# Order of the products in w_up: each 512-column product with the 256-column product of its tile behind it

## The reference

```python
h = rms_norm(x, norm_ffn_g[i])
u = causal_dwconv(h @ w_up[i], ffn_conv_w[i])      # w_up: 2048 x 11264, convolution of 3 taps
u_g, u_v = jnp.split(u, 2, axis=-1)
x = x + (jax.nn.silu(u_g) * u_v) @ w_down[i]       # w_down: 5632 x 2048
```

## Time and profile before

| | |
|---|---|
| time, median of 3 runs | 1561.92 us (1561.05 to 1563.58) |
| time of the profiled execution | 1562.31 us |
| its span, first to last instruction | 1560.6 us |
| TensorE products | 7667, busy 1552.0 us |
| w_up, first stretch | 736.0 to 1004.9 us |
| w_up, second stretch | 1131.4 to 1354.2 us |
| products of w_up | 1408 of 512 columns (L614), 1408 of 256 columns (L620) |

### The profile page before, as it was taken

One profiled execution on the slowest core, in us unless ns is written; L12 is line 12 of the kernel. 1 busy time (PEld: TensorE's weight loads), 2 busy tenths in 40 slices (PEclk: granted clock), 3 DMA queues, 4 the chain that ended last, 5 costly groups with the idle time before them and its releaser, 6 DMA issues.

```text
span 1560.6 us, 20864 instructions
## 1 busy us (share of the span) xinstructions
PE 1552.0 (99%) x7667; PEld 1311.8 (84%) x7667; DVE 1141.2 (73%) x1366; ACT 815.4 (52%) x970; POOL 80.4 (5%) x120
## 2 busy tenths in 40 slices
PE   9999999999999999999999999999999999999998
PEld 7878888888888888888888888888888888888887
DVE  5599867766676557678678778778767777787754
ACT  6355454544554445456555455555545555555543
POOL 5000110000000011000000101000000010000000
PEclk9999999999999999999999999999999999999999
DMA  7656655666655688665677767666677776575564
GB/s 256 209 169 193 195 175 175 189 183 194 196 179 173 200 233 256 205 204 195 200 219 226 215 217 242 206 221 222 218 213 214 207 224 215 193 231 192 189 199 150
DMA packets 167818, 319.66 MB, mean 205 GB/s; under 512 B 11287, under 2 KB 16131, under 8 KB 167744
## 3 DMA queue, kind: packets, MB, share of 16 engines
q1 hardware_dynamic: 159616, 300.59, 59.6%
q0 software_dynamic: 8096, 18.10, 6.1%
q10 hardware_dynamic: 32, 0.01, 0.0%
HBM read 316.55 MB, written 19.92 MB: 216 GB/s over the span
## 4 chain that ended last, share of the span: by engine, by line
PE 91%; DVE 4%; DMA 2%; ACT 1%; issue 1%; DVEq 0%; SPq 0%; ACTq 0%
PE psum L614 16%; PE psum L641 14%; PE psum L643 14%; PE psum L642 14%; PE psum L620 8%; PE psum L603 7%; PE psum L604 7%; PE psum L605 7%; DVE w_lo L1519 1%; DMA raw<-in_w_up 1%; ACT w_hi L1134 1%; PE psum L818 0%; PE psum L767 0%; DMA xtok<-in_x 0%; DVE cv L2049 0%
## 5 line engine op out<-in xcount | busy, mean ns | idle before, releaser
L1519 DVE TENSOR_TENSOR w_lo<-raw,w_hi 128x1024 fp32r<-128x1024 f32 x547 | 663.7, 1222 | 326.2 <-ACT w_hi L1134 323.8
L1134 ACT CAST w_hi<-raw 128x1024 fp32r<-128x1024 f32 x546 | 570.6, 1051 | 535.5 <-PE psum L643 296.3
L614 PE MATMUL psum<-h_both,w_hi 128*128 128x512 f32 x1408 | 336.7, 391 | 0.0
L641 PE MATMUL psum<-w_hi,h_both 128*128 128x512 f32 x844 | 332.1, 394 | 0.2 <-DVE h_both L1561 0.2
L643 PE MATMUL psum<-w_hi,h_both 128*128 128x512 f32 x844 | 328.7, 389 | 0.0
L642 PE MATMUL psum<-w_lo,h_both 128*128 128x512 f32 x844 | 328.5, 389 | 0.0
L614 PEld LDWEIGHTS psum<-h_both,w_hi 128*128 128x128 f32 x1408 | 258.5, 188 | 50.7 <-DVE w_lo L1519 0.4
L620 PEld LDWEIGHTS psum<-h_both,w_lo 128*128 128x128 f32 x1408 | 180.7, 191 | 8.2 <-DVE w_lo L1519 1.4
L643 PEld LDWEIGHTS psum<-w_hi,h_both 128*128 128x128 f32 x844 | 158.4, 188 | 33.3
L641 PEld LDWEIGHTS psum<-w_hi,h_both 128*128 128x128 f32 x844 | 158.5, 188 | 33.2 <-DVE h_both L1561 0.6
L642 PEld LDWEIGHTS psum<-w_lo,h_both 128*128 128x128 f32 x844 | 158.6, 188 | 31.8
(11 more groups left out here) (343 smaller groups left out, 1434.7 us busy)
## 6 DMA issues: line engine op xcount, KB each, us to landing
raw<-in_w_up SPq DMA_DIRECT2D x176, 512.0 KB, 4.5
raw<-in_w_gate SPq DMA_DIRECT2D x96, 512.0 KB, 4.0
raw<-in_w_in SPq DMA_DIRECT2D x89, 512.0 KB, 3.5
raw<-in_w_down SPq DMA_DIRECT2D x75, 512.0 KB, 4.6
raw<-in_w_ple_gate SPq DMA_DIRECT2D x32, 512.0 KB, 4.5
raw<-in_w_out SPq DMA_DIRECT2D x28, 512.0 KB, 4.8
raw<-in_w_moba_out SPq DMA_DIRECT2D x16, 512.0 KB, 4.5
first_sums<-in_w_down POOLq DMA_DIRECT2D x26, 256.0 KB, 5.3
```

The costliest lines, as they stand in the source:

```text
L614: mm = nc.tensor.matmul(wide[part][:, j, :], w_hi[:, c % RING, w], h_both[:, kt + k, :, :].rearrange("p h s -> p (h s)"), start=first and ...
L641: nc.tensor.matmul(o, sh, w_hi[:, c % RING, w], start=first and k == 0, stop=False, skip_group_check=True)
L1134: A.copy(w_hi[:, c % RING, :], raw[:, c % RING, :]).then_inc(chunk_high, 1)
L1519: V.tensor_tensor(w_lo[:, c % RING, :], raw[:, c % RING, :], w_hi[:, c % RING, :].bitcast(F32), ALU.subtract).then_inc(chunk_split, 1)
```

## The change

In a chunk each 512-column product is followed at once by the 256-column product of its own tile. The argument `low_first` and the two groups go; the last product of a chunk is always a 256-column one. The diff:

```diff
-        def wide_chunk(c, part, kt, first, last, low_first, i, step):
+        def wide_chunk(c, part, kt, first, last, i, step):
 
             pe.wait_ge(chunk_split, i * step + (c + 1))
             tiles = [(k, j, slice(k * W + j * P, k * W + (j + 1) * P)) for k in range(2) for j in range(QD)]
 
-            def joined():
-                for k, j, w in tiles:
-                    mm = nc.tensor.matmul(wide[part][:, j, :], w_hi[:, c % RING, w], h_both[:, kt + k, :, :].rearrange("p h s -> p (h s)"),
-                                          start=first and k == 0, stop=last and low_first and k == 1, skip_group_check=True)
-                return mm
-
-            def low():
-                for k, j, w in tiles:
-                    mm = nc.tensor.matmul(wide[part][:, j, S:2 * S], w_lo[:, c % RING, w], h_hi[:, kt + k, :],
-                                          start=False, stop=last and not low_first and k == 1, skip_group_check=True)
-                return mm
-
-            if low_first:
-                low()
-                mm = joined()
-            else:
-                joined()
-                mm = low()
+            for k, j, w in tiles:
+                nc.tensor.matmul(wide[part][:, j, :], w_hi[:, c % RING, w], h_both[:, kt + k, :, :].rearrange("p h s -> p (h s)"),
+                                 start=first and k == 0, stop=False, skip_group_check=True)
+                mm = nc.tensor.matmul(wide[part][:, j, S:2 * S], w_lo[:, c % RING, w], h_hi[:, kt + k, :],
+                                      start=False, stop=last and k == 1, skip_group_check=True)
             mm.then_inc(chunk_used, 1)
...
-                    wide_chunk(c0 + 8 * part + j, part, 2 * j, j == 0, j == 7, j % 2 == 1, i, 16)
+                    wide_chunk(c0 + 8 * part + j, part, 2 * j, j == 0, j == 7, i, 16)
```

## The result

| | before | changed |
|---|---|---|
| median | 1560.58 us (16 runs) | 1564.68 us (16 runs) |
| lowest to highest | 1558.57 to 1563.58 | 1563.07 to 1567.12 |
| span of the profiled execution | 1560.6 | 1561.3 |

The changed kernel takes 1.0027 times as long, interval 1.0019 to 1.0034: some 4.1 us slower, where the prediction's sum was -1.35 us. (Its three runs of the kernel before had a median of 1561.92 us; the sixteen here have 1560.58, so it is the difference that is to be compared.) The 1564.68 us lie outside the likeliest case of the prediction, 1559.5 to 1563.5 us, and inside the one of the rival "the 512s never settle", 1563.5 to 1571, near its lower end.

What follows compares the result with a forecast made beforehand. It took TensorE's product pace in w_up as the bound. Saving 1.75 us less 0.4 us gave -1.35 us; with the median 0.39 us below the profiled time, 1560.6 us was forecast, range 1551 to 1568 us (8 in 10).

Steps and rivals of the forecast that it cites:

- the likeliest case of the prediction: w_up: the per-product cost is fixed, so a pair takes 346.7 ns; 1559.5 to 1563.5 us, chance 0.46.
- the 512s never settle: w_up: only a run of 512s restores their pace, so alternating ones stay slow; +4.4 us, 1566 us, chance 0.28.
- the bounds of the pair: w_up: one 512 plus one 256 takes 337 to 354.4 ns, or far above, 366.7 ns.
- I take 346.7 ns: w_up: an alternating pair takes the sum of undisturbed products, 346.7 ns, against 347.9 ns before.
- -1.75 us for 88 periods: w_up: 0.020 us saved on each of 88 periods as changes of size stop costing, before a deduction of 0.4 us.
- The reason given for it: w_up: shortening going down in size and lengthening coming up cancel; the 13.3 ns on top belong to each product.
- The sign for it: w_up: a distance over 229 ns from a 512 to the 256 behind it would show unsettled 512s.
- the marks given with the rival: w_up: slower if a 512 exceeds about 229 ns with the 256 at 120, or 234 with it at 114.
- Bank (b): w_up: a 256 adds to the bank the product just ahead wrote; put between nothing and 2 ns, taken as nothing.
- last product (c): w_up: a chunk now always ends on a 256-column product; costed at nothing.
- The faster rival: w_up: weight loads hold 256s back and hide behind 512s; pair 337 to 342 ns, -6.6 to -12 us, chance 0.17.
- The fed-bound stretch: 826 to 936 us in w_up: weight preparation sets the pace, so 0.4 us of the saving does not count.

## Why the prediction was wrong

**What bounds the kernel, and the bounds of the pair.** Right. TensorE's pace is the time of w_up (226.2 us for 640 pairs, busy throughout), nothing else moved (w_down between the stretches takes 125.1 us before and 125.2 after, what follows the second stretch 206.4 and 206.5), and the pair came out inside the bounds given, 337 to 354.4 ns.

**The step that failed** is "I take 346.7 ns". The sum of undisturbed products is a pair's time in one rhythm, to a tenth of a nanosecond. But the same order has a second rhythm of 353.3 ns that holds as steadily, and the kernel was in that one for the whole second stretch in every profile of strict alternation, and for the first stretch in some. The term that followed, -1.75 us for 88 periods, would be -1.7 us if all is short and +7.6 us if all is long: 1408 pairs times -1.2 or +5.4 ns. The profile that is long in both stretches shows +5.7 and not 7.6, mostly because the kernel before lost some 1.6 us to late weights near 936 us, which neither profile of the changed kernel did. The measured +4.1 us lies between the profiles' +1.0 and +5.7, and the second stretch alone gives 3.4 of it.

**The reason given for it** was half right. The first product on the way up and the first on the way down do give and take the same 7 ns. What I held to be a thing of longer runs, the slow second and later 512s behind 256s, does not vanish when the runs do: in the long rhythm each three pairs pay 20 ns, the amount that a run of sixteen or eight pays once. (That it is the same thing that is paid is a guess from the equal amount.) This was the slower rival's mechanism (no 512 restores the state), with 0.28. Its price was put at 349.4 to 354.4 ns and its sum at +4.4 us, 1566 us: 353.3 ns is in it, the median 1564.68 us is within its range. That +4.4 is so near the measured +4.1 is luck: the profiles of the changed kernel show +1.0 and +5.7 us, and the median lies between them. The prediction held one mechanism or the other to be true of the whole kernel, and both came, one behind the other, in one execution.

**The sign for it** failed as worded: under "What would show it" a 512 of over 229 ns was to mean unsettled 512s. In the short rhythm the 512s take 230 ns and the pair is not slower for it, since the 256s take 117. Only the sum decides, as the marks given with the rival (229 with 120, 234 with 114) have it, and as does the time of a chunk: 8 x 353.3 ns = 2.83 us is in the 2.80 to 2.84 named for it.

**Bank (b) and last product (c).** Taken as nothing. For (b) the 346.7 ns of the short rhythm bear it out as a fixed price; whether the long rhythm has to do with the bank stays open. (c) was not tried by itself.

**The faster rival**, hidden loads, is refuted for the order tried. Each 512 behind a 256, as the objection had it, takes 230 ns or more, and no pair was under 346.7 ns in any order.

**The fed-bound stretch.** I took 0.4 us off because from 826 to 936 us a faster TensorE would wait longer at 935 us. In the profile shown the first stretch ran short and had no such wait at all; with one transpose ahead it ran short and waited 1.6 us; in the long rhythm it waited 1.2 us with each part entered from 256s and not at all in the changed kernel's repeat. So the wait doesn't follow the rhythm. What else sets it I didn't look for.

**What stays open.** Where the choice falls is shown: in every profile the rhythm changed only at a stall, at a wait or behind other products, and behind settled runs it was always the long one. What decides it there isn't shown; the same eight transposes were followed by either. What in TensorE makes a second steady pattern possible, whether it needs two products in a row on one bank, and why it is 20 ns for three pairs, isn't settled by these runs. Nor is how often each rhythm is taken in unprofiled runs.

## What to carry to other kernels

The pace of a row of products isn't the sum of what each takes among its like. Where two sizes follow in a short pattern, TensorE may have more than one steady rhythm for it, and behind a stall of some 60 ns one program can take either and keep it for over 200 us; so look at the distance over several periods, in every stretch and in more than one profile, before a price is put on the order. Runs of eight or sixteen of a size cost 20 ns for each change there and back but are the same in each stretch, and here that beat an order whose best case is 1.2 ns a pair better and whose other case is 5.4 ns worse.

## What the runs showed of the hardware that was not expected

- Strict alternation of 512 and 256 columns, each with a weight load of its own, has two steady paces at a granted clock of 1.00: 1.04 us and 1.06 us for three pairs. Each held for over 220 us while DMA and the other engines worked on (DMA share 0.74 and 0.69, VectorE busy for 77% and 75%).
- So two profiled executions of one program differ by 4.9 us, 4.6 of them in a stretch in which TensorE never waits. The kernel with eight transposes ahead ranged from 1560.3 to 1569.0 us; that the rhythm is the reason there too is likely and not shown.
- A change of size there and back costs 20 ns in runs of sixteen or eight, 17 ns in runs of four, 3 ns in runs of two.
